# Storing attention's output by feature, with halves added on GpSimd and the division by the sums moved into the routing stage

## The reference, cut to what matters

```python
# per set: 8 grouped-query heads (2 kv heads, 64 wide), then 8 latent-attention heads (64 + 32 wide, values 64)
sc = einsum('bqkgd,bskd->bkgqs', q, k) * scale
p = softmax(sc, axis=-1)
o = einsum('bkgqs,bskd->bqkgd', p, v)            # (tokens, head * 64)
o = concatenate([rms_norm(oa, out_norm_a), rms_norm(ob, out_norm_b)], axis=-1)   # each half (512) by its own mean square
x = x + einsum('bse,ed->bsd', o, w_o)
h2 = rms_norm(x, norm_ffn)
x = x + expert_choice_moe(h2, w_router, w_gate, w_up, w_down)    # 16 experts, each takes its best 64 tokens of a set
```

## Time and profile before

| | us |
|---|---|
| median of 3 runs | 1083.67 (1082.73 to 1084.68) |
| the profiled execution's own time | 1086.1 |
| its span, first to last instruction | 1083.7 |
| mean granted clock of TensorE | 0.986 |

### The profile page before, as it was taken

One profiled execution on the slowest core, in us unless ns is written; L12 is line 12 of the kernel. 1 busy time (PEld: TensorE's weight loads), 2 busy tenths in 40 slices (PEclk: granted clock), 3 DMA queues, 4 the chain that ended last, 5 costly groups with the idle time before them and its releaser, 6 DMA issues.

```text
span 1083.7 us, 16970 instructions
## 1 busy us (share of the span) xinstructions
PE 1044.8 (96%) x5689; PEld 896.7 (83%) x5689; DVE 886.0 (82%) x1147; ACT 775.3 (72%) x1095; POOL 423.3 (39%) x394
## 2 busy tenths in 40 slices
PE   8999999999999999998699999999999999999995
PEld 7999978999889987887578888888888888888884
DVE  6787669989999843338899999999999999999991
ACT  7655569888998843344577877877878878788771
POOL 2466576111358502334524432344323444234101
PEclk9999999999999999999799999999999999999998
DMA  8232050010211348741799999999999999999982
GB/s 305 79 116 102 1 197 1 2 41 20 98 41 40 98 109 263 225 164 79 235 417 378 398 400 400 400 421 400 401 400 400 413 408 401 400 400 406 415 310 39
DMA packets 77936, 266.05 MB, mean 245 GB/s; under 512 B 11249, under 2 KB 13516, under 8 KB 77628
## 3 DMA queue, kind: packets, MB, share of 16 engines
q1 hardware_dynamic: 69776, 239.68, 56.9%
q0 software_dynamic: 8048, 25.68, 8.3%
q10 hardware_dynamic: 60, 0.01, 0.0%
HBM read 239.07 MB, written 26.28 MB: 245 GB/s over the span
## 4 chain that ended last, share of the span: by engine, by line
PE 48%; DVE 2%; DMA 1%; issue 1%; ACT 0%; POOLq 0%; POOL 0%; DVEq 0%; ACTq 0%
PE ps L2003 10%; PE ps L2005 10%; PE ps L2004 10%; PE ps L2017 5%; PE ps L2019 5%; PE ps L2018 5%; PE ps L1980 1%; DMA xe<-h,idxT 1%; DMA out<-y,give 1%; DVE lo L2171 0%; DVE idx L1776 0%; DVE affT L1785 0%; DVE gates L1771 0%; ACT hi L2093 0%; POOLq L2274 0%
## 5 line engine op out<-in xcount | busy, mean ns | idle before, releaser
L2171 DVE TENSOR_TENSOR lo<-raw,hi 128x2048 fp32r<-128x2048 f32 x191 | 430.0, 2285 | 32.3 <-ACT hi L2093 32.0
L2093 ACT ACTIVATE hi<-raw 128x2048 fp32r<-128x2048 f32 x192 | 364.6, 1918 | 70.0 <-PE ps L2005 57.3
L2003 PE MATMUL ps<-hi,xehi 128*128 128x512 f32 x480 | 188.3, 392 | 1.3 <-DVE h L2193 1.0
L2005 PE MATMUL ps<-hi,xelo 128*128 128x512 f32 x480 | 186.9, 389 | 0.0
L2004 PE MATMUL ps<-lo,xehi 128*128 128x512 f32 x480 | 186.8, 389 | 0.0
L1939 POOL DMA_INDIRECT xe<-h,take x60 | 111.1, 1851 | 25.1 <-issue 13.7
L2003 PEld LDWEIGHTS ps<-hi,xehi 128*128 128x128 f32 x480 | 90.1, 188 | 20.2 <-issue 1.4
L2005 PEld LDWEIGHTS ps<-hi,xelo 128*128 128x128 f32 x480 | 90.1, 188 | 18.8
L2004 PEld LDWEIGHTS ps<-lo,xehi 128*128 128x128 f32 x480 | 90.2, 188 | 18.1
L1934 POOL COPY take<-idx 128x4 uint32 (+1 forms) x15 | 29.0, 1930 | 193.7 <-DVE xt L2187 187.4
L1361 DVE TENSOR_TENSOR probTlo<-ps,probThi 128x512 fp32r<-128x512 f32 x128 | 87.8, 686 | 12.1 <-ACT probThi L1318 10.0
(11 more groups left out here) (302 smaller groups left out, 2192.3 us busy)
## 6 DMA issues: line engine op xcount, KB each, us to landing
raw<-in_w_down SPq DMA_DIRECT2D x64, 1024.0 KB, 10.0
raw<-in_w_gate SPq DMA_DIRECT2D x60, 1024.0 KB, 9.7
raw<-in_w_up SPq DMA_DIRECT2D x60, 1024.0 KB, 9.3
w_raw<-in_w_in SPq DMA_DIRECT2D x8, 592.0 KB, 9.0
x<-in_x SPq DMA_DIRECT2D x8, 512.0 KB, 3.7
woraw<-in_w_o SPq DMA_DIRECT2D x4, 1024.0 KB, 5.1
o<-attention_out SPq DMA_DIRECT2D x8, 512.0 KB, 4.4
xr<-in_x SPq DMA_DIRECT2D x8, 512.0 KB, 7.0
```

The lines of the kernel that those rows point to most:

```text
L2003: pe.matmul(ps[:, dst[n], :], rowhi[:, c, :], hi[w][:, cols], start=c == 0, stop=False)
L2005: last = pe.matmul(ps[:, dst[n], :], rowlo[:, c, :], hi[w][:, cols], start=False, stop=c == KD - 1)
L2093: act.activation(hi[s][:], raw[s][:], ACT.Copy).then_inc(hi_done, 1)
L2171: dve.tensor_tensor(lo[s][:], raw[s][:], hi[s][:].bitcast(F32), ALU.subtract).then_inc(lo_done, 1)
```

## The change

`turn_output`, `halves`, L1374, L1377 and the row stores go. In their place: `ot` has two buffers. SP moves rows 64 to 127 of `ot` down to rows 0 to 63 of a ring of three tiles `sums` (a transfer on chip), GpSimd adds the upper half to it (`add_halves`), and SP stores the sum by feature. The reciprocals are made once per set for all 64 columns, turned by one transpose, and stored. `route` loads a tile by feature, with its reciprocals spread over the partitions, and VectorE multiplies them (`normalise`). No transpose of `o` is left. The squares are one instruction over the tile, GpSimd adds them over the chunks (`group_sums`), and two products with a column of ones give the sums (`group_squares`).

```diff
@@ attend, SP
+        def move_half(g):
+            sp.wait_ge(ot_copied, g + 1)
+            if g >= OUT_RING:
+                sp.wait_ge(o_stored[g % OUT_RING], STORED + 16 * (g // OUT_RING))
+            sp.dma_start(att["sums"][g % OUT_RING], att["ot"][g % 2][VD:P, :].rearrange("d (i t) -> d i t", i=TS)).then_inc(
+                ot_moved[g % 2], 16)
+        def store_head(g):
+            s, h = g // HEADS, g % HEADS
+            sp.wait_ge(o_added, g + 1)
+            sp.dma_start(o_dram[TS * s:TS * (s + 1), h % 2 * VD:(h % 2 + 1) * VD, h // 2, :].rearrange("i p t -> p i t"),
+                         att["sums"][g % OUT_RING]).then_inc(o_stored[g % OUT_RING], 16)
+        for g in range(ALL):
+            move_half(g)
+            store_head(g)
+            if g == HEADS - 1:
+                load_output_weights(0)
+                load_output_weights(1)
+                store_reciprocals(0)
+            elif g == HEADS + 3:
+                load_output_weights(2)
+            elif g == HEADS + 6:
+                load_output_weights(3)
+            elif g == ALL - 4:
+                route_first(sp, g + 1)
+            elif g == ALL - 3:
+                route_second(sp)
+        store_reciprocals(1)
+        route_rest(sp)
@@ attend, GpSimd
+        def add_halves(g):
+            lower = att["sums"][g % OUT_RING]
+            pool.wait_ge(ot_moved[g % 2], MOVED + 16 * (g // 2 + 1))
+            pool.tensor_tensor(lower, lower, att["ot"][g % 2][0:VD, :].rearrange("d (i t) -> d i t", i=TS), ALU.add).then_inc(o_added, 1)
-        split_after = {HEADS + GROUP: (0, 1), HEADS + QH: (2, 3), HEADS + QH + 1: (4,), HEADS + QH + 2: (5,),
-                       HEADS + QH + 3: (6,), HEADS + QH + 4: (7,)}
+        split_at = {HEADS + 2: 0, HEADS + 3: 1, HEADS + 4: 2, HEADS + 6: 3, HEADS + QH: 4, HEADS + QH + 1: 5,
+                    HEADS + QH + 3: 6, HEADS + QH + 4: 7}
+        for g in range(GROUP, ALL):
+            if g in keys[2:]:
+                split_values(g)
+            if g in copies:
+                copy_rotary_keys(g)
+            if g in split_at:
+                split_output_weights(pool, split_at[g])
+            add_halves(g - 2)
+        add_halves(ALL - 2)
+        group_sums(0)
+        add_halves(ALL - 1)
@@ attend, TensorE
-        def turn_output(g, i): ...
+        def turn_reciprocals(s): ...                  # one transpose, at u = HALF + 4 and NU + 2
@@ attend, ScalarE
                 act.wait_ge(pv_done, TS // 2 * (g + 1))
-                if g:
-                    act.wait_ge(o_ready, g)
-                act.activation(ot[:], ps[:, OT_BANK, :], ACT.Copy).then_inc(ot_copied, 1)
+                if g >= 2:
+                    act.wait_ge(o_added, g - 1)
+                act.activation(ot[g % 2][:], ps[:, OT_BANK, :], ACT.Copy).then_inc(ot_copied, 1)
@@ attend, VectorE
-                dve.reciprocal(rsum, ...); dve.tensor_tensor(pj[:, :, h * VD:(h + 1) * VD], ..., ALU.mult)
+            if u == NU - 3:
+                normalise(0, 0)
+            elif u == NU - 1:
+                o_low(0, 0)
+            elif u == NU:
+                normalise(0, 1)
@@ route, SP
     def load_rows(sp, j):
+        t = ORDER[j]
+        if j >= 2:
+            sp.wait_ge(otlo_done, 2 * (j - 1))
+            sp.wait_ge(osq_done, j - 1)
+            sp.wait_ge(o_ready, 2 * j)
+        sp.dma_start(o[j % 2][:], o_dram[t]).then_inc(o_loaded[j % 2], 16)
+        for half in range(2):
+            sp.dma_start(r[min(j, 1)][half * VD:(half + 1) * VD], r_dram[t // TS, t % TS, half].partition_broadcast(VD)).then_inc(
+                r_loaded[min(j, 1)], 16)
+    def wait_for_stores(sp, heads, sets): ...        # all stores of these heads and sets have landed
+    def sync_first(sp, heads):
         sp.wait_ge(wo_lo, KD)
+        wait_for_stores(sp, heads, 1)
         load_rows(sp, 0)
@@ route, GpSimd
+        def group_sums(j):
+            squares = osq[:].rearrange("p (g c) t -> p g c t", g=2)
+            pool.wait_ge(osq_done, j + 1)
+            steps.did(pool.tensor_tensor(squares[:, :, 0:2, :], squares[:, :, 0:2, :], squares[:, :, 2:4, :], ALU.add))
+            steps.wait()
+            if j:
+                pool.wait_ge(ss_ready, j)
+            pool.tensor_tensor(acc[:], squares[:, :, 0, :], squares[:, :, 1, :], ALU.add).then_inc(acc_done, 1)
@@ route, TensorE
+        def group_squares(j):
+            pe.wait_ge(acc_done, j + 1)
+            for n in range(2):
+                last = pe.matmul(SS[:, 2 * j + n:2 * j + n + 1], acc[:, n, :], k["ones"][:], start=True, stop=True)
+            last.then_inc(ss_ready, 1)
-                    if j + 1 < T and c in (2, 5) and (j or c > 2):
-                        o_transposes(j + 1, c // 3)
+                    if j == 0 and c == GROUP_CHUNKS:
+                        group_squares(0)
+                    if j + 1 < T and c == KD - 1:
+                        group_squares(j + 1)
@@ route, VectorE: ahead of o_low(j + 1, 0) in each turn
+                normalise(j + 1, 0)
+                normalise(j + 1, 1)
+                group_means(j)
```

More of the change, by code:

```diff
@@ L251, in build @@
         att["v"] = [bm(f"v{i}", [P, TS, 2, VD], F32R) for i in range(2)]
-        att["ot"] = bm("ot", [P, SEQ])
+        att["ot"] = [bm(f"ot{i}", [P, SEQ]) for i in range(2)]
+        att["sums"] = [pj[0:VD, :, C_CQ + r * P:C_CQ + (r + 1) * P] for r in range(OUT_RING)]
         assert bm.at <= w_in_end, (bm.at, w_in_end)
@@ L1119, in gpsimd_program, with split_values @@
         keys = [g for kind, g in preps if kind == "k"]
-        pool.wait_ge(proj_done, T)
-        for n, g in enumerate(keys):
+        def split_values(g):
+            n = keys.index(g)
             wait_for_rows(pool, g)
@@ L1216, in values, with turn_reciprocals @@
             last.then_inc(pv_done, 1)
-        def turn_output(g, i):
-            if i == 0:
-                pe.wait_ge(ot_copied, g + 1)
-                if g:
-                    pe.wait_ge(o_done, g)
-                else:
-                    pe.wait_ge(halves_ready, 1)
-            dst, cols = ps[:, O_BANK, i * VD:(i + 1) * VD], slice(i * P, (i + 1) * P)
-            turned = pe.matmul(dst, ot[:, cols], k["halves"][:], start=True, stop=True)
-            if i == TS - 1:
-                turned.then_inc(o_ready, 1)
+        def turn_reciprocals(s):
+            pe.wait_ge(rsum_done, s + 1)
+            pe.transpose(ps[0:HEADS * TS, R_BANK, s * P:(s + 1) * P],
+                         att["sum"][:, s * HEADS * TS:(s + 1) * HEADS * TS], k["ident"][:]).then_inc(r_turned, 1)
         first_key()
@@ L1241, in tensor_program @@
             turned = u - 3 if 0 <= u - 3 < NU else None
-            output = (u - 11) // TS if u >= 11 and (u - 11) % TS == 0 else None
-            for i in range(TS):
-                if output is not None:
-                    turn_output(output, i)
-                if turned is not None:
+            if turned is not None:
+                for i in range(TS):
                     transpose_prob(turned, i)
@@ new lines, in group_root, with rest @@
+        def group_root(j):
+            pool.wait_ge(sso_done, j + 1)
+            pool.tensor_tensor(ro(j), sso(j), k["minus_half"][:, 0:2], ALU.pow).then_inc(ro_done, 1)
+        def rest():
+            for i in range(2):
+                pool.memset(aff[i][:], 0.0).then_inc(aff_cleared, 1)
+            group_root(0)
+            group_sums(1)
+            pool.wait_ge(small_loaded, 16 * (QUARTERS + 1))
+            pool.tensor_tensor(wr[:], wr[:], k["gcol"][:, G_FFN:G_FFN + KD].unsqueeze(2).to_broadcast([P, KD, EXPERTS]),
+                               ALU.mult).then_inc(wr_scaled, 1)
+            for j in range(1, T + 1):
+                if j < T:
+                    group_root(j)
+                u = j - 1
+                if u == LAST:
+                    pool.wait_ge(ss2_done, T + 1)
+                    steps.did(pool.tensor_tensor(ss2(u), last_sums[:, 0:1], last_sums[:, 1:2], ALU.add))
+                    steps.wait()
+                else:
+                    pool.wait_ge(ss2_done, u + 1)
+                inverse_root(r2(u), ss2(u), D, r2_done)
+                pool.dma_start(out_rows[ORDER[u]], x1[u % 2][:]).then_inc(x1_stored[u % 2], 16)
+                if j + 1 < T:
+                    group_sums(j + 1)
+                pool.wait_ge(h2_scaled, u + 1)
+                if u >= LAST - 1:
+                    pool.wait_ge(aff_done, u + 1)
+                pool.tensor_tensor(h2[u % 2][:], h2[u % 2][:], gffn[:], ALU.mult).then_inc(h2_done, 1)
+                pool.wait_ge(h2_done, u + 1)
+                pool.dma_start(h2_rows[ORDER[u]], h2[u % 2][:]).then_inc(h2_stored[u % 2], 16)
@@ L1823, in rest @@
             add_second(LAST - 2)
+            normalise(LAST, 0)
+            normalise(LAST, 1)
+            group_means(LAST - 1)
             o_low(LAST, 0)
```

291 lines of the change are left out of this document (136 added, 155 removed).

## The result

The changed kernel took 1099.47 us (median of 4 runs, 1097.99 to 1102.67), the kernel before, on the same chip, 1083.26 (4 runs). The ratio is 1.0152 with a 95% interval of 1.0124 to 1.0179: slower by 16 us where 10 of gain were forecast.

A forecast was written before the change was run, and what follows sets the result against it. TensorE (PE) was taken as the bound, until another engine is late. Gains 11.2 + 5.5 + 2.0 + 3.0 = 21.7 less losses 3.3 + 1.5 + 5.7 + 1.0 = 11.5 gave net 10.2: 1073.5 us, range 1068 to 1079.

The forecast's parts named there:

- Latent heads, 0.70 each: Attention's latent heads: dropping `turn_output` and transposes saves PE 0.70 us per head, 11.2 for 16, all of it counting.
- Grouped-query heads: Two attention stretches: gains of 2.5 and 3.0 us; in the second, GpSimd's late additions cost 3.3 (bounds 0 and 4.7).
- The second rival: Grouped-query heads: ACT is the bound at once, gains there 0 instead of 5.5, 1079 us; chance 0.13.
- Second latent stretch: Heads 22 to 28: ACT's copy for head 28 waits 2.9 us for GpSimd, 1.5 reaching PE (bounds 0 and 2.9).
- Tile 0's rows: Step 125: VectorE waits 7 us (4.8 to 9.0) for tile 0's load, PE stops 5.5; loss 5.7 (bounds 2 and 9).
- the spread reciprocals behind it about 1.0: Tile 0's load: reciprocals land about 1.0 us behind o, ending the chain 17.3 after copy 28.
- Tile 4 and the start of routing: Third tile in order: reciprocals at T + 18.6, PE idles 3.2 us instead of 2.2; loss 1.0 (bounds -2 and 4).
- Move and addition bring the store to T + 4.6: Tile 4, T being head 31's copy of `ot`: the store comes 4.6 us after it, as the old way did.
- Routing's gain: Turns 1 to 6: 0.9 us of transposes less 0.3 for one-column products, 0.6 each; 3.0 in all after turn 0.
- The later turns: Routing: squares' sums are ready at 12.6 us, PE comes at 13.7; fits by 1.1, nothing lost.
- the third rival: End of turns 1 to 6: the turn's chain becomes the bound, 1.8 us per turn, 1086 us; chance 0.13.
- so what comes before can start earlier and carry the end with it, one for one: Experts: PE busy 520 of 533 us, ACT waits for weights only 1.9, so earlier savings move the end equally.

The follow-up runs named there:

- e7_128: The kernel before with an unused allocation of 128 bytes, putting the weight ring 128 past a multiple of 256: 1091.10 us, ratio 1.0067 to the kernel before.
- e4_adds: From e1_base, GpSimd's addition of halves put ahead of the split of w_o in the same turn: 1089.33 us, 1.0053 to the kernel before.
- e1_base: The changed kernel with the column of ones held in a 256-byte allocation, so later tiles lie at their old addresses: 1089.67 us, 1.0051 to the kernel before.
- e3: From e1_base, tile 0's row loads issued one head earlier, behind head 26's store instead of head 28's: 1086.27 us, 1.0021 to the kernel before.
- e6: From e3 with some w_o splits moved: tile 4's rows loaded ahead of the norm's gain, router weights ahead of both: 1080.00 us.
- e8: From e6, tile 1's loads issued behind head 30's move, and GpSimd's sums for tile 0 ahead of head 30's addition: 1078.04 us.
- e2_shift: The kernel before with an unused allocation of 320 bytes, putting the weight ring 64 past a multiple of 256: 1090.95 us, 1.0063 to the kernel before.

## Why the prediction was wrong, step by step

The forecast difference at the experts' first product was -10.2 us. With the old addresses it was +7.1 (531.4 to 538.5), so 17.3 were missed there, and 7.6 behind it (559.9 for 552.3). The bullets below place these from one profile of each kernel, and the start of the experts varies by up to 3 us between profiles (e7_128 above).

- **Latent heads, 0.70 each: right.** Copies 6 to 14 lose 5.5 us in eight heads, with PE full.
- **Grouped-query heads: right in the first stretch, wrong in the second.** The first lost 2.5 as forecast. In the second a gain of 3.0 against a loss of 3.3 should have left +0.3; it was +3.3. ACT's waits came as forecast (1.14, 1.22, 2.37 for 1.0, 1.3, 2.4). Missed: 3.0. e4_adds doesn't divide it between a smaller gain and a dearer lateness: the stretch came back to before's length (gain 0), but with a stop of 2.15 us for GpSimd's v in it, so that the gain may have been up to 2.1 and the lateness cost up to 5.4, more than its upper bound of 4.7. A term the prediction lacked is v itself, made by GpSimd behind the splits. The second rival (ACT as the bound) is not shown: ACT was busy 86% of the stretch, not above 95%.
- **Second latent stretch: the wait was right, its price was not.** ACT's copy for head 28 waited 2.6 us (2.24 in e1_base) for 2.9 forecast. Between the first scores behind copy 22 and the last ahead of the stop, 30 scores in both, PE took 56.4 us before and 54.9 in e1_base. Seven `turn_output` are gone there, 4.9 us, but only 1.5 came. So some 3.4 were lost where 1.5 were taken: to the rotary key's copy, which stands behind the splits and additions (1.4), and behind the late copies for heads 25 and 28. Missed: 2.
- **Tile 0's rows: mechanism right, size wrong.** VectorE stood 11.0 us, beyond the bound of 9.0. Its data was there 18.6 us after copy 28 and not 17.3: the failed step is "the spread reciprocals behind it about 1.0", as `r` lands 5.6 us after its own issue. VectorE arrived after 7.6, not 8.3. And the 7 was taken between a case with lateness and one without, while the lateness came. From there the sum holds: 11.0 + 1.3 - 2.8 = 9.5 for PE, which stopped 9.98 (9.68 in e1_base) instead of 5.5. Behind it TensorE ran at half clock, granted 0.50 from 384 to 388 and 0.57 to 390 in e1_base, about 2.4 us of loss for 1.2 taken. From copy 22 to copy 31 the forecast was +1.6 and e1_base shows +8.3: 6.7 missed, of which 2 stand in the bullet above and 4.2 are the stop, so that about 0.5 is left for the clock less what the tail gave back.
- **Tile 4 and the start of routing: the failed step is "Move and addition bring the store to T + 4.6".** The move of head 30 sat behind tile 1's loads, so the last store was issued at T + 7.9 (404.73), tile 4's reciprocals at T + 15.0, and they were there at T + 24.1, not T + 18.6. The chain behind them took 7.8 for 7.2. In e1_base PE stopped 5.45 there and 2.0 at three smaller waits for GpSimd, 7.5 in all, and lost about 2.4 us to half clock; the kernel before had 2.2 and about 1.5 (granted 0.52, then 0.63, from 408 to 412). That is 6.2 of loss where 1.0 was taken: missed 5.2. e3, e6 and e8 shorten these stops or take them away, as loads are put elsewhere in the same queue.
- **Routing's gain: 0.42 per turn, not 0.6.** The exponentials of the first full turn are 14.15 apart, 14.58 before. The four one-column products take 0.47 with their switch, not 0.3, and the turns from the second tile's exponentials to the last's gave 1.7 us, not 3.0 net: missed 1.3.
- **The later turns fit,** as the prediction had it, and the third rival, its only slow case, did not happen: in the changed kernel PE never waits at the end of a turn after the second. Slower came from tiles 0 and 4 and the experts instead.
- **The experts: "so what comes before can start earlier and carry the end with it, one for one" was the largest single miss,** 7.6 us. The prediction named the condition (experts of another time than 1083.7 - 531.4 prove it wrong), but had no term for an allocation's shift.

The missed parts, 3.0 + 6.7 + 5.2 + 1.3, come to 16.2 of the 17.3. The rest isn't placed. Nor is the 2.5 us by which the changed kernel's experts begin later than e1_base's (541.05 for 538.51), in one profile each.

The Trainium skill ("SBUF — State Buffer", section "Who interferes with whom") was cited for VectorE operations with two SBUF inputs and GpSimd operations that read SBUF, which by it exclude each other. Here are two `o_low` of one turn, the second beside a GpSimd operation that reads SBUF, the first alone, then that GpSimd operation:

```profile
436.28 0.69 DVE L1791 TENSOR_TENSOR otlo<-o,othi 128x512 fp32r<-128x512 f32 x1 [1.95 <-ACT othi L1711]
...
442.10 1.22 DVE L1791 TENSOR_TENSOR otlo<-o,othi 128x512 fp32r<-128x512 f32 x1
```

```profile
441.48 1.29 POOL L1555 TENSOR_TENSOR osq<-osq 128x512 f32<-128x512 f32 x1 [4.87 <-ACT osq L1717]
442.85 1.07 POOL L1559 TENSOR_TENSOR acc<-osq 128x256 f32<-128x256 f32 x1
```

0.69 becomes 1.22, and GpSimd's L1559 takes 1.07, where at 401.38 us, alone, it took 0.72. When the second `o_low` started, 0.67 us of the GpSimd operation were left, and it took 0.53 longer; at 456.55 and 470.87, with 0.36 left, it took 0.23 and 0.21 longer. The added time grows with what is left of the other operation, as the rule has it, if waiting counts in the recorded duration. It stayed within the slack of 1.1 us, as the prediction said. The prediction's remark that L1377 and the maxima are the same length beside the splits can't be read from the earlier trace rows, which have one length each, but the trace before bears it out: 0.42 to 0.43 us for L1377, 0.68 to 0.69 for the maxima.

## What to carry to other kernels

When an edit adds, drops or resizes an on-chip allocation, compare the addresses of everything behind it, and time the kernel with the old ones before believing any other explanation; a pad of a few bytes is the cheapest experiment there is. A small transfer costs its 2.4 us only in an empty queue: behind 1.5 MB it cost 7.0 to 7.8, and GpSimd stood up to 11.2 us for it; so order a queue by who waits, and put bulk loads behind the small moves that gate other engines. And when a wait is taken away, look for the next one in the same stretch before reading a bound from it: in e4_adds a stop that the profile put down to nothing was GpSimd's next late product.

## What the runs showed of the hardware that was not expected

Loads of 1 MB of down weights into a ring at a multiple of 256 bytes per partition landed in 10.0 us, and 64 bytes past one in 13.2 (128 past one gave waits of 54.9 us for them, 47.7 in e2_shift), with the number and sizes of the packets unchanged between before and e2_shift (77,936 and 266.05 MB); the experts' time went from 552.3 to 559.7 us, while the rate that the profile shows from 600 to 1000 us fell by under 3%, from 405 to 395 GB/s. Why the address matters no run shows. The time from one expert to the next was 33.5 us before throughout; in the changed kernel and in e2_shift it was so for about five experts and then 34.6. And 256 KB of reciprocals, spread over partitions from rows of 4 KB, took 5.6 us from issue to landing between 372 and 400 us, 6.4 in the whole run.
